# One column group a call: the value matmuls of the sampled sequences write 32 partitions by 512 columns instead of 128 partitions by 256

## The reference

```python
s = jnp.einsum("bqhmd,bkhmd->bhmqk", q, k) * (DH_D ** -0.5)      # 256 cached keys and the 4 new ones
s = jnp.where(k_pos[None, :] <= q_pos[:, None], s, -jnp.inf)
p = jax.nn.softmax(s, axis=-1)
a = p[:, :, 0] - lam * p[:, :, 1]
o = jnp.einsum("bhqk,bkhv->bqhv", a, v)                          # per head: 4 queries x 260 keys x 128 channels
return rmsnorm(o, subln) * (1.0 - lambda_init)
```

## Time and profile before

| | |
|---|---|
| time, median of 3 runs | 1744.99 us (1741.71 to 1745.56) |
| profiled execution | 1741.71 us |
| its span | 1739.9 us |
| TensorE busy | 1667.5 us, 96% of the span |
| VectorE, ScalarE busy | 762.4 us, 556.0 us |
| mean granted TensorE clock | 0.985 |
| stage "sample" | about 1077 to 1143 us of the span |

### The profile page before, as it was taken

One profiled execution on the slowest core, in us unless ns is written; L12 is line 12 of the kernel. 1 busy time (PEld: TensorE's weight loads), 2 busy tenths in 40 slices (PEclk: granted clock), 3 DMA queues, 4 the chain that ended last, 5 costly groups with the idle time before them and its releaser, 6 DMA issues.

```text
span 1739.9 us, 30651 instructions
## 1 busy us (share of the span) xinstructions
PE 1667.5 (96%) x12834; PEld 1576.0 (91%) x12834; DVE 762.4 (44%) x1151; ACT 556.0 (32%) x847; POOL 4.3 (0%) x20
## 2 busy tenths in 40 slices
PE   7999999999999899999999998869999999999996
PEld 7999999999987667999999965659999999999996
DVE  4333333333862433643346587534444333333332
ACT  5222222222333323522111275353234222222222
POOL 0000000000000000000000000000000000000000
PEclk9999999999999999999999999989999999999998
DMA  5232323322333820333333230722322222333221
GB/s 130 83 86 86 88 87 96 91 85 58 76 79 96 263 78 15 83 86 98 85 94 97 90 131 25 269 71 81 88 85 86 84 84 86 91 89 101 84 84 52
DMA packets 253837, 161.77 MB, mean 93 GB/s; under 512 B 8235, under 2 KB 246048, under 8 KB 253763
## 3 DMA queue, kind: packets, MB, share of 16 engines
q1 hardware_dynamic: 253616, 160.67, 31.7%
q10 hardware_dynamic: 146, 0.04, 0.0%
HBM read 143.14 MB, written 16.40 MB: 92 GB/s over the span
## 4 chain that ended last, share of the span: by engine, by line
PE 87%; DVE 4%; ACT 3%; DMA 3%; issue 1%; SPq 1%; ACTq 0%; DVEq 0%
PE ps L395 71%; PE ps L765 3%; PE ps L953 2%; PE ps L917 1%; PE ps L1241 1%; PE ps L1169 1%; DMA pages<-in_cache_k 1%; PE ps L1112 1%; PE ps L1002 1%; PE ps L1285 1%; PE ps L1391 1%; DVE small L2264 1%; PE ps L1097 1%; DMA Cb<-in_state_C 1%; PE ps L1166 0%
## 5 line engine op out<-in xcount | busy, mean ns | idle before, releaser
L395 PE MATMUL ps<-xn_hi,w_hi 128*128 128x272 f32 (+1 forms) x2208 | 639.6, 290 | 5.9 <-DVE w_lo L369 2.6
L395 PE MATMUL ps<-xn_hi,w_lo 128*128 128x272 f32 (+1 forms) x2208 | 641.4, 291 | 0.0
L395 PE MATMUL ps<-xn_lo,w_hi 128*128 128x272 f32 (+1 forms) x2208 | 638.4, 289 | 0.0
L365 ACT ACTIVATE w_hi<-raw 128x1024 fp32r<-128x1024 f32 (+1 forms) x200 | 222.2, 1112 | 822.9 <-PE ps L395 819.7
L395 PEld LDWEIGHTS ps<-xn_hi,w_hi 128*128 128x128 f32 x2208 | 416.0, 188 | 8.0 <-DVE w_lo L369 3.3
L395 PEld LDWEIGHTS ps<-xn_hi,w_lo 128*128 128x128 f32 x2208 | 415.7, 188 | 0.0
L395 PEld LDWEIGHTS ps<-xn_lo,w_hi 128*128 128x128 f32 x2208 | 414.8, 188 | 0.0
L369 DVE TENSOR_TENSOR w_lo<-raw,w_hi 128x1024 fp32r<-128x1024 f32 (+1 forms) x200 | 257.6, 1289 | 225.9 <-ACT w_hi L365 225.5
L395 PE MATMUL ps<-h_lo,w_hi 128*128 128x280 f32 (+1 forms) x704 | 204.7, 291 | 0.0
L395 PE MATMUL ps<-h_hi,w_hi 128*128 128x280 f32 (+1 forms) x704 | 204.7, 291 | 0.0
L395 PE MATMUL ps<-h_hi,w_lo 128*128 128x280 f32 (+1 forms) x704 | 204.6, 291 | 0.0
(11 more groups left out here) (356 smaller groups left out, 2022.5 us busy)
## 6 DMA issues: line engine op xcount, KB each, us to landing
raw<-in_w_in SPq DMA_DIRECT2D x56, 512.0 KB, 3.9
raw<-in_ffn_w_gate SPq DMA_DIRECT2D x44, 512.0 KB, 3.8
raw<-in_ffn_w_up SPq DMA_DIRECT2D x44, 512.0 KB, 3.8
raw<-in_ffn_w_down SPq DMA_DIRECT2D x32, 704.0 KB, 4.5
Cb<-in_state_C SPq DMA_DIRECT2D x32, 256.0 KB, 4.1
out<-Cb SPq DMA_DIRECT2D x32, 256.0 KB, 3.1
pages<-in_cache_k SPq DMA_DIRECT2D x16, 512.0 KB, 4.6
pages<-in_cache_v SPq DMA_DIRECT2D x16, 512.0 KB, 5.2
```

The source lines that it names most:

```text
L365: act.activation(w_hi[s][:, 0:p.nk, :], raw[s][:, 0:p.nk, :], ACT.Copy).then_inc(hi_done[s], 1)
L395: mm = pe.matmul(ps[:, bank + half, 0:p.half], w[s][:, k, :], x[:, k0 + k, cols], start=first and k == 0 and a == 0, stop=last and k == p. ...
```

## The change

In `values`, a call now makes two passes (half) of three matmuls (g). Each takes 512 value channels as its moving operand. The output of sequence b goes to the partitions 32(b % 4) to 32(b % 4) + 32, the channels 0 to 511 to bank 6 and the channels 512 to 1023 to bank 7. A call makes 6 matmuls instead of 12. `back_out` reads accordingly: head h's channels lie in one 128-column block after the transposes, and the columns of the four sequences are 32 apart. The copy to `osb`, the transposes and all semaphores stay.

```diff
@@ values
-                c0 = 256 * (b % 2)
-                for g in range(3):
-                    for j in range(4):
-                        w = (pages[:, page_slot((1, b)), g, 256 * j:256 * j + 256] if g < 2
-                             else vtok[:, 5, 256 * j:256 * j + 256])
-                        mm = pe.matmul(ps[32 * j:32 * j + 32, 6 + b % 4 // 2, c0:c0 + 256], AT3[:, b % 2, g, :], w,
-                                       start=g == 0, stop=g == 2)
+                r0 = 32 * (b % 4)
+                for half in range(2):
+                    for g in range(3):
+                        w = (pages[:, page_slot((1, b)), g, 512 * half:512 * half + 512] if g < 2
+                             else vtok[:, 5, 512 * half:512 * half + 512])
+                        mm = pe.matmul(ps[r0:r0 + 32, 6 + half, :], AT3[:, b % 2, g, :], w, start=g == 0, stop=g == 2)
                 mm.then_inc(sv_full, 1)
@@ back_out
                 for h in range(HD):
-                    c0 = 128 * (h % 2) + 32 * (h // 2) + 4 * h
-                    src = wide(6, 128, D).rearrange("p (b k) -> p b k", b=4)[:, :, c0:c0 + 4]
-                    c = v.tensor_copy(qkv[:, h, NP_ + 16 * r:NP_ + 16 * r + 16].rearrange("p (b t) -> p b t", t=DSEQ), src)
+                    src = ps[:, 6 + h // 4, 128 * (h % 4):128 * (h % 4) + 128].rearrange("p (b k) -> p b k", b=4)
+                    c = v.tensor_copy(qkv[:, h, NP_ + 16 * r:NP_ + 16 * r + 16].rearrange("p (b t) -> p b t", t=DSEQ),
+                                      src[:, :, 4 * h:4 * h + 4])
```

## The result

The changed kernel takes 1764.29 us (median of 4, 1762.53 to 1765.59) against 1745.28 us before (median of 4, 1741.71 to 1749.67): a ratio of 1.0107, 95% interval 1.0082 to 1.0133, slower by 19.0 us. The forecast was 1764 us, slower. The profiled execution of the changed kernel took 1767.12 us, its span 1765.3; it is the slowest of this kernel's five and not in the median, while the profiled one of the kernel before is the fastest of its four.

A forecast was written before the change was run, and what follows sets the result against it. TensorE was taken to bound most of the kernel, key-cache pages narrowly the changed stage. +21.5 us of stretch less 1.6 us of clock gave +19.9 us, from the median 1764.9, stated as 1764 us; range 1756 to 1772.

The forecast's parts named there:

- The slack: Stage "sample", steady turns: late key pages set the pace, leaving TensorE about 0.76 us free per turn.
- The price of a record: In values: each 512-column record costs 0.43 us with no overlap, so a call takes 5.2 us instead of 1.44.
- The upper end: In values: 0.475 us a record, from a pair of 512-column records, making a call 5.7 us.
- The sum: First values call to osb copy: turns of 9.03 us, stretch 68.93 us instead of 47.46, +21.5 us.
- The DMA share: First values call to osb copy: DMA engines' busy share falls from 0.75 to near 0.5.
- The clock: back(1) and the next stage: TensorE idles less, so the clock stays up; gain 1.6 us, bounds 0 and 2.3.
- The first heads: Next stage's sub-norm sums: squares waiting for the first two heads come about 1.4 us sooner; half counted, 0.7.
- Everything before 1092 us as it is: Stages ahead of "sample": expected unchanged in the changed profile.
- A: In values: neighbouring records in two banks overlap two by two, call 3.15 us, kernel 1748.5 us; chance 0.04.
- B: In values: a record costs a fixed slot, so half as many pay; kernel 1744 us; chance 0.03.
- C: Stage "sample": the clock falls to half throughout, call 10.4 us, +77 us, kernel 1822 us; chance 0.05.

The follow-up runs named there:

- e6: Kernel before the change with every values call issued twice (24 matmuls of 256 columns): 1746.00 us, ratio 1.0019.
- e5: Changed kernel with every values call issued twice (12 matmuls of 512 columns): 1803.41 us (one time).
- e1: Changed kernel with the two halves alternating between banks 6 and 7, always the same 32 partitions: 1764.77 us (one time).
- e2: Changed kernel with the bank 7 half sent to a different column group and the halves alternating, plus extra small copies in back_out: 1748.10 us, ratio 1.0024.
- e3: Kernel before the change with only the loops swapped, so three matmuls in a row write the same 32 partitions: 1744.83 us, ratio 1.0008.
- e4: Kernel before the change with 17 extra transposes into an unused bank in the last turn, where TensorE waits: 1741.56 us, ratio 0.9990.
- e7_two_outer: e2 with its loops swapped, so all six records of one column group come before the six of the other: 1750.20 us (one time).

## Why the prediction was right

- **The slack.** That a turn has 0.76 us free and no more was read from waits and the timeline. e6 bears it out: 10.2 us more of matmul, 4.0 us more of stretch. So does e5, where nothing was free: 41.2 and 41.2.
- **The price of a record.** 0.43 us was taken from 256-column records, and 0.43 it is. A call was put at 5.2 us and takes 5.24. The upper end, 0.475 from the pair of 512-column records, has its like in the last two records of a call, which also take 0.95 us, paid once a call as assumed. The ratio to the packed call is 5.24/1.44 = 3.6 for four column groups. The estimate from the Trainium skill ("TensorE: Matmul & The Clock Gate", part 3), 3.4 us a call, came from its 2.38 for three tiles and was too low here.
- **What the change puts in a row.** Three runs tell the parts of the edit apart. Bank order: nothing (e1). 512-column records: nothing (e2, where alternating column groups bring the call to 2.68 us). 256-column records of one group put in a row: 2.77 us instead of 1.44 (e3), held there by the overtaking. One column group for the whole call: everything. By groups at work the call takes 1.44 (four), 2.68 (two), 5.24 us (one).
- **The sum.** Turn 9.03 predicted, 9.08 measured; stretch 68.93 and 69.40; 0.3 us of the difference is the 0.04 of a call, eight times. Nothing else moved: the eight copies with the other step take 0.71 and 0.74 us where they took 0.72 and 0.74. The DMA share was to be 0.5 and is 0.56.
- **The clock.** Gain put at 1.6 us with bounds 0 and 2.3; behind the `osb` copy it measured 2.49 in this execution, a little over the upper bound. Of this, `back(1)` (0.9) is shown by e4. The first heads brought 1.5 where 1.4 was the full price. They were counted half because they might fail, and they do fail in e1_banks and e4_warm. What decides it stays open.
- **What was luck.** The mechanism and the call were right by their own numbers. That forecast and median are 0.3 us apart says less: the stretch was 0.5 too short, the clock gain in the profiled execution 0.9 too small, the two errors point opposite ways, and the executions of one kernel spread over 5 to 8 us.
- **"Everything before 1092 us as it is"** was wrong for the profiled execution, by 5.95 us of loads and of clock behind them. The medians have no sign of it.
- **The rivals.** A fell with e1. B fell with the 592 ns records at 0.43 us. Its argument, that packed records stand 0.06 us apart whatever their columns, was a misreading: in the first full turn of before, 16 score records of 288 columns take 0.97 us and 16 values records of 256 columns 0.87, so they too go by columns. C fell with the clock at 1.00 from the first values call of the changed kernel to the last.

## What to carry to other kernels

In all these runs a record with 32 weight columns held its column group for a time that went by its moving columns, 0.215 us for 256 and 0.43 for 512. Halving the number of matmuls by giving all of them the same output partitions costs the side-by-side running: look at the distance of the starts, not at the records' length or the number of instructions. What such a loss does to the end is read from the slack of that loop, the waits that it can still eat; beyond these it goes through one to one (e5).

## What the hardware showed that was not expected

- Records don't always start in program order. For a free column group they start ahead of waiting ones: in e3_order and e7_two_outer two page records of the next group precede the first `vtok` record of the group before, and the calls take 2.77 us instead of an expected 4.5, and 3.56 instead of 4.75. So the sentence on the kernel before, that each engine runs its instructions in the order in which they are written, doesn't hold for TensorE's records.
- With TensorE equally busy up to the same point, the granted clock of the first head of the next stage was full in the changed kernel (1.18 us for four records) and half in e1_banks (2.21 us). To the table load the two executions differ by 1.9 us. The kernels differ only in the order of six matmuls, but there is one trace of each, so whether the order or the execution decides isn't shown.
